# Compression products turned over: inputs loaded, weights streamed, and the output product placed between the first scores

## The reference, cut to what matters

```python
def compress(kv, pe, w1, w2):
    NC = (T - CMP_BLOCK) // CMP_STRIDE + 1          # 31 windows of 512 tokens
    blocks = kv[:, :, idx, :] + pe
    flat = blocks.reshape(B, G, NC, CMP_BLOCK * dh) # 2048 long
    return jax.nn.silu(flat @ w1) @ w2              # 2048 x 128, then 128 x 64

kc = rmsnorm(compress(heads(kcm, KVH), cmp_pe[i, 0], cmp_w1[i, 0], cmp_w2[i, 0]), nsa_knorm_g[i, 0])
vc = compress(heads(vcm, KVH), cmp_pe[i, 1], cmp_w1[i, 1], cmp_w2[i, 1])
s_cmp = jnp.einsum('bgntd,bgcd->bgntc', q_nope, kc) * scale
```

## Time and profile before

| | |
|---|---|
| median of 3 runs | 2836.83 us (2835.43 to 2836.85) |
| the profiled execution | 2835.33 us, span 2833.5 us |
| busy | PE 2738.7, POOL 1386.1, ACT 1272.8, DVE 1173.3 us |
| granted TensorE clock, mean | 0.989 |

### The profile page before, as it was taken

The page is one execution under the profiler, slowest core; times in us unless marked ns, Lnnn a source line. Parts: engine busy times, 40 slices in busy tenths (PEclk is TensorE's granted clock), DMA queues, the critical chain, the costliest instruction groups (busy, mean ns, idle before and its releaser), DMA issues.

```text
span 2833.5 us, 41633 instructions
## 1 busy us (share of the span) xinstructions
PE 2738.7 (97%) x13748; PEld 2292.0 (81%) x13748; DVE 1173.3 (41%) x2138; ACT 1272.8 (45%) x2187; POOL 1386.1 (49%) x1713
## 2 busy tenths in 40 slices
PE   8999899999989999999999999999999999999998
PEld 6889668788966878888888888888888788888887
DVE  4768752577775234432242321323442224242232
ACT  5554644655564552544443432324354544343233
POOL 4535444553544444454553655555455454365553
PEclk9999999999899999999999999999999999999999
DMA  5213003322301232233332333334223343233332
GB/s 151 71 50 88 26 24 97 87 68 56 96 9 34 86 107 82 75 96 106 107 109 67 98 104 90 100 95 115 71 79 105 97 125 91 60 112 98 96 97 97
DMA packets 270820, 242.47 MB, mean 86 GB/s; under 512 B 29376, under 2 KB 203648, under 8 KB 270592
## 3 DMA queue, kind: packets, MB, share of 16 engines
q1 hardware_dynamic: 267696, 235.12, 28.6%
q10 hardware_dynamic: 2896, 4.52, 0.5%
HBM read 237.51 MB, written 2.10 MB: 85 GB/s over the span
## 4 chain that ended last, share of the span: by engine, by line
PE 67%; issue 17%; POOL 13%; DVE 1%; ACT 1%; DMA 0%; POOLq 0%; DVEq 0%; ACTq 0%
PE bank L1988 11%; PE bank L1992 11%; PE bank L1991 11%; POOL wlo L2832 11%; PE bank L1922 8%; PE bank L1926 8%; PE bank L1925 8%; PE bank L1877 2%; PE bank L841 1%; PE bank L845 1%; PE bank L844 1%; PE bank L2113 1%; PE bank L2079 1%; POOL vv L2821 0%; POOL Ql L2821 0%
## 5 line engine op out<-in xcount | busy, mean ns | idle before, releaser
L2832 POOL TENSOR_TENSOR wlo<-raw,whi 128x256 fp32r<-128x256 f32 (+1 forms) x1616 | 1291.5, 832 | 1303.2 <-ACT whi L2137 1303.0
L2137 ACT CAST whi<-raw 128x1024 fp32r<-128x1024 f32 (+2 forms) x443 | 455.4, 1034 | 600.8 <-PE bank L1988 401.9
L1922 PE MATMUL bank<-xhi,whi 128*128 128x512 f32 x928 | 364.2, 392 | 1.8 <-DVE h L2524 1.6
L1926 PE MATMUL bank<-xhi,wlo 128*128 128x512 f32 x928 | 361.4, 389 | 0.0
L1925 PE MATMUL bank<-xlo,whi 128*128 128x512 f32 x928 | 361.4, 389 | 0.0
L1988 PE MATMUL bank<-whi,xhi 128*128 128x512 f32 x832 | 326.5, 392 | 3.9 <-DVE xlo L2415 3.9
L1992 PE MATMUL bank<-whi,xlo 128*128 128x512 f32 x832 | 324.0, 389 | 0.0
L1991 PE MATMUL bank<-wlo,xhi 128*128 128x512 f32 x832 | 323.8, 389 | 0.0
L841 PE MATMUL bank<-whi,xhi 128*128 128x512 f32 (+2 forms) x672 | 246.7, 367 | 5.5 <-DVE pT L1497 3.1
L845 PE MATMUL bank<-whi,xlo 128*128 128x512 f32 (+2 forms) x672 | 242.2, 360 | 0.0
L844 PE MATMUL bank<-wlo,xhi 128*128 128x512 f32 (+2 forms) x672 | 242.1, 360 | 0.0
(11 more groups left out here) (509 smaller groups left out, 4966.0 us busy)
## 6 DMA issues: line engine op xcount, KB each, us to landing
raw<-in_w_in SPq DMA_DIRECT2D x147, 512.0 KB, 3.7
raw<-in_w SPq DMA_DIRECT2D x132, 512.0 KB, 3.8
raw<-in_w_pg SPq DMA_DIRECT2D x16, 512.0 KB, 3.8
raw<-in_w_o SPq DMA_DIRECT2D x16, 512.0 KB, 3.8
raw<-in_xa_k SPq DMA_DIRECT2D x16, 512.0 KB, 3.9
raw<-in_xa_v SPq DMA_DIRECT2D x16, 512.0 KB, 3.8
raw<-in_xa_q SPq DMA_DIRECT2D x16, 512.0 KB, 3.8
raw<-in_xa_o SPq DMA_DIRECT2D x16, 512.0 KB, 3.8
```

The costliest lines, as they stand in the source:

```text
L1922: mm = pe.matmul(o, wh, rhs[0][:, k, :], start=(k == 0), stop=False)
L1926: mm = pe.matmul(o, wl, rhs[0][:, k, :], start=False, stop=(k == KD - 1))
L2137: nc.scalar.copy(whi[:, j % SLOTS, 0:nk * cols], raw[:, j % SLOTS, 0:nk * cols]).then_inc(hi_split, 1)
L2832: ins = nc.gpsimd.tensor_tensor(wlo[:, s, part], raw[:, s, part], whi[:, s, part].bitcast(F32), ALU.subtract)
```

## The change

Four edits go together.
- `step_c_hid` gives TensorE the inputs (62 columns) as the loaded operand and streams the 128 columns of the weights; the result has 62 partitions and 128 columns. The `gate` on ScalarE and the product on VectorE work on 62 x 128 instead of 128 x 62, and VectorE writes to a place of its own, `hidr`.
- A new step `("c_flip", w)` transposes `hidr` back on TensorE into bank 1, and VectorE copies 128 x 62 to `hid`.
- `("c_flip", 0)` stands before `q_rope`; `("c_flip", 1)` behind fill 0.
- `c_out` stands behind score 0 and exp 0, `c_key` behind score 1, `("c_score", 0)` behind exp 1 and recip 0, `("c_exp", 0)` behind score 2 and fill 1; `nz_gate` 1 follows `nz_exp` 1 directly.

```diff
@@ -296,15 +296,18 @@
     hid = [[("c_hid", w, i, (f"cmp_w1_{w}", 8 * i, 8, 0, P)) for i in range(2)] for w in range(2)]
     s += kc[:1] + [("q_root",)] + kc[1:] + nz[:1] + [("q_norm",), ("k_norm",), ("z_gate", 3)] + nz[1:2]
     s += [("c_in", 0), ("k_pair",), ("c_in", 1)] + nz[2:] + [("hg_turn", h) for h in range(HG)] + [("nz_exp", 0)]
-    s += hid[0][:1] + [("nz_gate", 0), ("q_rot",)] + hid[0][1:] + [("k_turn",)] + hid[1][:1] + [("q_rope",)] + hid[1][1:]
-    s += [("nz_exp", 1), ("c_out",), ("nz_gate", 1)]
+    s += hid[0][:1] + [("nz_gate", 0), ("q_rot",)] + hid[0][1:] + [("k_turn",)] + hid[1][:1] + [("c_flip", 0), ("q_rope",)] + hid[1][1:]
+    s += [("nz_exp", 1), ("nz_gate", 1)]
     main, last = attention_steps()
-    main.insert(1, ("c_key",))
+    i = main.index(("score", 2))
+    assert main[:i] == [("score", 0), ("c_score", 0), ("exp", 0), ("score", 1), ("c_exp", 0), ("exp", 1), ("recip", 0)]
+    main[:i] = [("c_flip", 1), ("score", 0), ("exp", 0), ("c_out",), ("score", 1), ("c_key",), ("exp", 1), ("recip", 0), ("c_score", 0)]
+    main.insert(main.index(("score", 2)) + 1, ("c_exp", 0))
     for gate, before in ((("nz_exp", 2), ("exp", 1)), (("nz_exp", 3), ("exp", 2)), (("nz_gate", 2), ("weigh", 1)), (("nz_gate", 3), ("weigh", 2))):
         main.insert(main.index(before), gate)
     out0 = tm("out0", "w_out", 0, 512, tiles=HG, k0=HG)
     out1, pg1 = tm("out1", "w_out", 512, 512), tm("pg1", "w_pg", 512, 512)
-    place(main, ("score", 0), [("fill", 0, FILL[0])], ahead=True)
+    place(main, ("c_flip", 1), [("fill", 0, FILL[0])], ahead=True)
     place(main, ("score", 2), [("fill", 1)])
     place(main, ("turn", 2), [("fill_add", 0), ("fill_add", 1)], ahead=True)
     place(main, ("value", 33), [("fill", 2)])
@@ -382,6 +385,8 @@
         return ([(("pe",), HIGH)] if step[1] == 0 else []) + [(("ct", step[1], g), HIGH) for g in range(NKV)]
     if kind == "c_hid":
         return [(("ch", step[1]), (0,))] if step[2] == 0 else []
+    if kind == "c_flip":
+        return [(("cf", step[1]), (1,))]
     if kind == "c_out":
         return [(("co",), HIGH)]
     if kind == "c_key":
@@ -616,6 +621,7 @@
         ce = kdx[:, 0:NH * NCMP].rearrange("p (h c) -> p h c", h=NH)
         pcT = et[0:32, :, :]
         hid = Ql[:, 0, 0:4 * NCMP].rearrange("p (w c) -> p w c", w=2)
+        hidr = Ql[:, 0, P:3 * P].rearrange("p (w n) -> p w n", w=2)
         kcn = Ql[:, 1, 0:P].rearrange("p (g d) -> p g d", g=NKV)
         vc = eB[0:32, 256:256 + P].rearrange("p (g d) -> p g d", g=NKV)
         kcT = eB[:, 384:512]
@@ -1046,21 +1052,28 @@
                 if i == 0:
                     pe.wait_ge(*clo_ready.next(l))
                     pe.wait_ge(*G.free(name, l))
-                o = G.ps(name)[:, 0:2 * NCMP]
+                o = G.ps(name)[0:2 * NCMP, 0:P]
                 for j in range(8):
                     a, b = (x[:, 8 * i + j].rearrange("p g c -> p (g c)") for x in ((chi0, clo0), (chi1, clo1))[w])
                     wh, wl = whi[:, s, j * P:(j + 1) * P], wlo[:, s, j * P:(j + 1) * P]
-                    mm = pe.matmul(o, wh, a, start=(i == 0 and j == 0), stop=False)
+                    mm = pe.matmul(o, a, wh, start=(i == 0 and j == 0), stop=False)
                     if j == 0:
                         mm.then_inc(chunk_begun, 1)
-                    pe.matmul(o, wh, b, start=False, stop=False)
-                    mm = pe.matmul(o, wl, a, start=False, stop=(i == 1 and j == 7))
+                    pe.matmul(o, a, wl, start=False, stop=False)
+                    mm = pe.matmul(o, b, wh, start=False, stop=(i == 1 and j == 7))
                 if i == 1:
                     mm.then_inc(*G.full(name))
 
+            def step_c_flip(step):
+                w = step[1]
+                name = ("cf", w)
+                pe.wait_ge(*G.evacuated(("ch", w), l))
+                pe.wait_ge(*G.free(name, l))
+                pe.transpose(G.ps(name)[:, 0:P], hidr[:, w, :], ident[:, :]).then_inc(*G.full(name))
+
             def step_c_out(step):
                 for w in range(2):
-                    pe.wait_ge(*G.evacuated(("ch", w), l))
+                    pe.wait_ge(*G.evacuated(("cf", w), l))
                 pe.wait_ge(*G.free(("co",), l))
                 for w in range(2):
                     for g in range(NKV):
@@ -1145,7 +1158,7 @@
                      "fm": step_fm, "tm": step_tm, "p_turn": step_p_turn, "hg_prep": step_hg_prep,
                      "hg_level": step_hg_level, "hg_same": step_hg_same, "hg_out": step_hg_out, "hg_turn": step_hg_turn,
                      "q_norm": step_q_norm, "q_rope": step_q_rope, "k_turn": step_k_turn, "c_in": step_c_in,
-                     "c_hid": step_c_hid, "c_out": step_c_out, "c_key": step_c_key, "c_score": step_c_score, "c_turn": step_c_turn, "c_val": step_c_val,
+                     "c_hid": step_c_hid, "c_flip": step_c_flip, "c_out": step_c_out, "c_key": step_c_key, "c_score": step_c_score, "c_turn": step_c_turn, "c_val": step_c_val,
                      "score": step_score, "turn": step_turn, "value": step_value}
             for step in steps1:
                 if step[0] in table:
@@ -1170,7 +1183,7 @@
                 link(nc.scalar.activation(x, x, ACT.Ln, bias=1.0))
                 return nc.scalar.activation(x, x, ACT.Exp, scale=-1.0)
 
-            def gate(name, cols=T, src=None, scale=-1.0):
+            def gate(name, cols=T, src=None, scale=-1.0, rows=P):
 
                 i = n_et[0] % 2
                 n_et[0] += 1
@@ -1179,13 +1192,13 @@
                 if src is None:
                     eu[i] = G.evacuated(name, l)
                     act.wait_ge(*G.filled(name, l))
-                    src = G.ps(name)[:, 0:cols]
+                    src = G.ps(name)[0:rows, 0:cols]
                 else:
                     n_read[0] += 1
                     eu[i] = et_read[0].at(l, n_read[0])
                     act.wait_ge(*G.evacuated(name, l))
-                nc.scalar.activation(et[:, i, 0:cols], src, ACT.Exp, scale=scale).then_inc(*sigs["act_step"].up())
-                one_over(et[:, i, 0:cols]).then_inc(*sigs["ex"].up())
+                nc.scalar.activation(et[0:rows, i, 0:cols], src, ACT.Exp, scale=scale).then_inc(*sigs["act_step"].up())
+                one_over(et[0:rows, i, 0:cols]).then_inc(*sigs["ex"].up())
 
             def square_place():
 
@@ -1401,7 +1414,7 @@
 
             def step_c_hid(step):
                 if step[2] == 1:
-                    gate(("ch", step[1]), 2 * NCMP)
+                    gate(("ch", step[1]), P, rows=2 * NCMP)
 
             def step_c_out(step):
                 place = square_place()
@@ -1767,8 +1780,14 @@
             def step_c_hid(step):
                 if step[2] == 1:
                     name = ("ch", step[1])
-                    e = et_place()[:, 0:2 * NCMP]
-                    tt_(hid[:, step[1], :], e, G.ps(name)[:, 0:2 * NCMP], ALU.mult).then_inc(*G.empty(name))
+                    rows = slice(0, 2 * NCMP)
+                    e = et_place()[rows, 0:P]
+                    tt_(hidr[rows, step[1], :], e, G.ps(name)[rows, 0:P], ALU.mult).then_inc(*G.empty(name))
+
+            def step_c_flip(step):
+                name = ("cf", step[1])
+                dve.wait_ge(*G.filled(name, l))
+                nc.vector.tensor_copy(hid[:, step[1], :], G.ps(name)[:, 0:2 * NCMP]).then_inc(*G.empty(name))
 
             def step_c_out(step):
                 place = sq[0:NCMP, n_sq[0] % 2, 0:P]
@@ -1857,7 +1876,7 @@
                      "forget_early": step_forget_early, "forget_late": step_forget_late, "tm": step_tm, "p_turn": step_p_turn, "hg_prep": step_hg_prep,
                      "hg_level": step_hg_level, "hg_kv": step_hg_kv, "hg_out": step_hg_out, "hg_turn": step_hg_turn,
                      "q_root": step_q_norm, "q_rot": step_q_rot, "q_rope": step_q_rope, "k_norm": step_k_norm, "k_turn": step_k_turn, "c_in": step_c_in,
-                     "c_hid": step_c_hid, "c_out": step_c_out, "c_score": step_c_score, "c_weigh": step_c_weigh,
+                     "c_hid": step_c_hid, "c_flip": step_c_flip, "c_out": step_c_out, "c_score": step_c_score, "c_weigh": step_c_weigh,
                      "score": step_score, "recip": step_recip, "weigh": step_weigh, "turn": step_turn, "y_part": step_y_part}
             for step in sums_behind(followed(steps1)):
                 if step[0] in table:
```

## The result

The changed kernel takes 2840.65 us, median of 20 runs (2838.42 to 2843.66), the kernel before 2835.39 in 20 runs beside it (2830.65 to 2839.97): ratio 1.0020, 95% interval 1.0014 to 1.0026. It is 5.3 us slower, where 1.5 us less was forecast. The profiled execution took 2843.66 us, at a mean granted clock of 0.988 (0.989 before). It is the longest of the 20, while the profiled one of the kernel before (2835.33) lies at the median there, so the two traces differ by more than the medians do.

What follows compares the result with a forecast made beforehand. It took waits on VectorE's gate product, then a chain of small steps to ("turn", 1), as the bound, not TensorE's 97%. Layer 0 1.55 us later, layer 1 3.05 earlier: 1.5 less than 2836.83, 2835.3; range 2830 to 2841.

Steps and rivals of the forecast that it cites:

- M: Start of the second gate product on VectorE; forecast at 291.3 in layer 0, as before, and 777.3 in layer 1, 4.0 earlier.
- The faster first 48 products: ("c_hid", 0, *) at 0.06 us each ends sooner, worth nothing: TensorE then idles some 6 us for VectorE's gate product.
- M to ("turn", 1): Stretch from M to that step's start on TensorE: 17.6 us without clock loss, 19.75 with it.
- Gate 0.67: nz_gate 1 on VectorE, behind nz_exp 1 and ahead of the ("c_flip", 1) copy, was to take 0.67 us.
- 2.15 low clock: TensorE idles 3.5 us between c_out and score 1; the low clock after it costs 1.3 to 3.0 us, middle 2.15.
- The rest of M to score 3: c_out's group evacuated at M+6.9, freeing bank 5 for score 1; score 3 starts at M+13.8 without clock loss.
- The sum: Layer 0 1.55 us later, layer 1 3.05 earlier at ("turn", 1): together 1.5 us less.
- TensorE as the bound: Rival: the 192 products save 10 to 20 us and the 3.2 before c_out go too; about 2820, chance 0.08.
- Pace unchanged: Rival: ("c_hid", 1, 0) takes 5.1 us instead of 2.6, M 2.5 later in each layer; 2840.3, chance 0.12.
- the prediction's outer range: 2830 to 2841 us: the forecast's own 2832 to 2838, widened to take in Clock up and Pace unchanged.
- Clock up: Rival: the clock stays up in the gap before score 1, ("turn", 1) at M+17.6; 5.8 us gained, 2831.0, chance 0.12.
- The slower rival: Low clock holds from the wait for VectorE's gate product through fill 0; 6.0 us lost, 2842.8, chance 0.10.

Runs made afterwards that it cites:

- the own bank: Second hidden product in bank 1 instead of 0: on the kernel before, ratio 0.9997; on turned products in the order of before, transposes in bank 3, 0.9983.
- four edits against those waits: Changed kernel with fill 1, then nz_gate 1, behind c_out, and own banks for c_out, c_key, transposes of p and second hidden product: 2823.12 us, ratio 0.9957.

## Why the prediction was wrong

**Where M lies** was right. The products start 0.06 us apart at full clock and 0.107 at the low one, TensorE idles over 6 us in both layers, and M falls 22.09 us behind the first product (forecast 22.1 and 21.8). Layer 0 gained nothing there and layer 1 3.8 us, which it had lost to the clock: in the trace of the kernel before the low level held from 759.6 to 786.9, 27.3 us, over M and beyond, in the changed one 6.8 us. Whether the kernel before does this in every execution isn't shown; it was profiled once. The faster first 48 products gave nothing, as said.

**Why two terms from M on failed.** M to ("turn", 1) was to be 19.75 us and was 23.11 and 22.17. Of the excess of 3.4 and 2.4 us:

- "Gate 0.67": the step took 2.40 and 2.42 us, 1.7 more per layer. The run with GpSimd held back shows the cause, not just the size. The row of 0.67 was true but was taken where the two engines met another way. In the kernel before, nz_gate 1 came at 295.32, and there it was GpSimd's instruction that waited, 2.96 us instead of the 2.34 that vlo took in the run with vhi held back:

```profile
293.31 1.90 POOL L2811 TENSOR_TENSOR vhi<-vv,zero 128x1024 fp32r<-128x1024 f32 x1
295.28 2.96 POOL L2814 TENSOR_TENSOR vlo<-vv,vhi 128x1024 fp32r<-128x1024 f32 x1
```

  Moving nz_gate 1 by 2.1 us put it into vhi. The Trainium skill, "SBUF — State Buffer", section "SBUF: two separate sides", says that a GpSimd operation that reads SBUF and a VectorE operation with two SBUF inputs take a shared port pair as an exclusive lock, each for its whole instruction. The runs agree: 2.40 against 0.69 for VectorE, 2.35 against 1.88 for GpSimd.
- "2.15 low clock", from a stretch of 3.4 to 6.8 us: it was 13.65 and 10.24 us long. From score 1 to score 3 went 10.74 and 9.79 us (changed) and 6.9 by the sum, 3.8 and 2.9 lost instead of 2.15. The step also had the clock fall in the wrong place, in the 3.5 us between `c_out` and score 1. In the changed kernel it fell at 294.5, inside the 2.48 us ahead of `c_out`, and at 789.5, in `c_out` itself, so the gap that the prediction named lay wholly inside the low stretch. With the wait ahead of `c_out` cut to 0.86 us it fell at 294.2 and 782.3, at the end of `c_out`, for 10.24 and 13.65 us, at a cost of 3.03 and 4.35. With no wait ahead of `c_out` (nz_gate 1 behind it) it fell at 295.7, inside the 3.67 us ahead of score 1, for 10.24. The length and the price are shown, and that useless work in the gap takes the price away. Which of the short waits behind M brings the clock down, and why it then stays down for 10 us and more, stays open.

The rest of M to score 3 (`c_out` evacuated 6.9 behind M) held: 6.78 with GpSimd out of the way.

**The sum.** In the stretch, both layers together, the changed kernel is 4.6 us slower (89.5 against 84.9, one execution each) where 1.5 less was forecast. 3.5 of the 6.1 us between are the gate and 2.4 the clock. The timed difference, 5.3 us, is of that size. The two profiled executions differ by 8.3; the remaining 3.7 lie outside the stretch, 3.4 us more of low clock at 680.3 (above) and 3.4 at 318.5 among them, which by estimate cost at most half their length each, and I did not separate them further. The longest of 20 executions was profiled here, so this part says little of the change.

**The rivals.** TensorE as the bound: 12 us less of its work made the kernel slower. Pace unchanged: no, the products start 0.06 us apart; that its 2840.3 lies beside the measured 2840.65, and that 2840.65 is inside the prediction's outer range of 2830 to 2841, is luck, since neither of the two rivals that widen it to that, clock up and pace unchanged, happened. Clock up: it would have been 17.59, and took useless products to get. The slower rival, the low clock through fill 0, did not happen in the changed kernel, where it ended before fill 0 (fill 0 at full pace, 286.76 to 289.84). It did with the old products: 27.3 us in layer 1 of the kernel before, most of fill 0 included, and 17.07 us, up to ("c_hid", 1, 1), in an execution of that kernel with the own bank. That the turned products prevent it, as its "against" had it, fits the narrower spread with them: in the order of before with the own bank, 2826.7 to 2831.3 with turned products against 2825.9 to 2841.8 with the old ones. The trace of the turned one has four stretches of 6.83 us in the two layers and none longer. It is one pair of kernels, and their ratios (0.9983 and 0.9997) have intervals that overlap.

## What to carry to other kernels

A duration from the trace belongs to what the other engines did beside it: before an instruction is moved, look what it will stand beside, GpSimd above all when both operands lie in SBUF. Price an idle stretch of TensorE by its length and by what the matmuls behind it lose, and put useful work into it: here the second part, 3 to 4 us a layer, cost more than the change was to bring, and in one layer the clock fell with no single wait over 1.7 us since fill 0. A product made faster off the path gives nothing until the waits on the path go; with four edits against those waits the same products were worth some 7 us.

## What the hardware showed that I had not expected

- TensorE stayed at granted clock 0.50 (1.2 GHz) through 17.0 us without a pause, 83 matmuls of the old products and transposes; in another execution of the same kernel the last 6.6 us before `("c_hid", 1, 1)` was done, 59 matmuls, ran at 1.00.
- With 24 products whose results nobody reads, low stretches of 10.24 and 13.65 us did not occur, and the time was 5.7 us less.
- A start 0.04 us after GpSimd's cost VectorE 1.7 us, a start 0.13 us before it cost GpSimd 0.47. In the kernel before, VectorE won although its record begins 0.04 us after GpSimd's, so records this close don't tell who comes first.
